# Second mixer of a two-layer encoder: key norms spread as fp32r pairs, the last value block bank by bank, six unread products at the first statistics

## The reference

```
x = x + 0.5 * swiglu(rms_norm(x, ffn1_norm[layer]), ...)
x = x + mixer(rms_norm(x, mix_norm[layer]), ...)      # layer 0: Hyena and windowed attention; layer 1: RWKV-7
x = x + 0.5 * swiglu(rms_norm(x, ffn2_norm[layer]), ...)
```

```
r, k, v = xr @ w_r, xk @ w_k, xv @ w_v
decay, a = f(xw @ w1 @ w2), sigmoid(a0 + xa @ a1 @ a2)          # per direction, low rank
kk = k * k_k                                                    # 16 heads of 64 channels
kk = kk / max(norm(kk over the 64 channels of a head), 1e-12)
k_dir, b_dir = k * (1 + (a - 1) * k_a), kk * a                  # per direction
S = S * w + (S @ -kk) outer b_dir + v outer k_dir               # scan over positions, both directions
```

## Time and profile before

| | us |
|---|---|
| median of 3 runs | 1233.02 |
| lowest and highest | 1231.18, 1236.94 |
| the profiled execution | 1231.86 |
| its span in the trace | 1230.1 |

### The profile page before, as it was taken

One profiled execution on the slowest core, in us unless ns is written; L12 is line 12 of the kernel. 1 busy time (PEld: TensorE's weight loads), 2 busy tenths in 40 slices (PEclk: granted clock), 3 DMA queues, 4 the chain that ended last, 5 costly groups with the idle time before them and its releaser, 6 DMA issues.

```text
span 1230.1 us, 27474 instructions
## 1 busy us (share of the span) xinstructions
PE 1198.3 (97%) x11198; PEld 1085.7 (88%) x11198; DVE 793.2 (64%) x1259; ACT 654.7 (53%) x1116; POOL 403.3 (33%) x218
## 2 busy tenths in 40 slices
PE   8999999998999999999999989998999999999998
PEld 6899999877889999998999979987999889999998
DVE  7655554787585555575555569969777758755554
ACT  5545454655274454475445446684666654554452
POOL 0343433212113434423443410006344412344433
PEclk9999999999999999999999989999999999999999
DMA  9345455422254554555455444421000025554452
GB/s 364 123 187 191 168 204 201 155 106 99 108 198 173 193 191 169 203 206 205 168 190 190 171 151 155 167 92 54 3 4 3 3 75 190 205 201 176 182 202 89
DMA packets 18657, 188.04 MB, mean 153 GB/s; under 512 B 2064, under 2 KB 2576, under 8 KB 3600
## 3 DMA queue, kind: packets, MB, share of 16 engines
q1 hardware_dynamic: 18576, 186.87, 41.3%
HBM read 185.82 MB, written 1.05 MB: 152 GB/s over the span
## 4 chain that ended last, share of the span: by engine, by line
PE 83%; DVE 10%; ACT 5%; issue 1%; DMA 0%; SPq 0%; DVEq 0%; ACTq 0%
PE gu_bank L267 24%; PE gu_bank L269 12%; PE bank L246 7%; PE bank L248 7%; PE bank L247 7%; PE bank L1493 7%; PE gu_bank L246 3%; PE gu_bank L1493 3%; PE gu_bank L247 3%; PE gu_bank L248 3%; DVE WL L201 2%; PE gu_bank L1524 2%; ACT WH L189 2%; DVE HX L407 1%; PE bank L949 1%
## 5 line engine op out<-in xcount | busy, mean ns | idle before, releaser
L210 POOL TENSOR_TENSOR WL<-raw,WH 128x1024 fp32r<-128x1024 f32 x96 | 325.8, 3393 | 587.9 <-ACT WH L195 566.4
L267 PE MATMUL gu_bank<-HX,WH 128*128 128x512 f32 x1280 | 455.7, 399 | 1.1 <-DVE PL L548 1.1
L269 PE MATMUL gu_bank<-HX,WL 128*128 128x256 f32 x1280 | 359.5, 281 | 0.0
L201 DVE TENSOR_TENSOR WL<-raw,WH 128x2048 fp32r<-128x2048 f32 (+1 forms) x113 | 242.8, 2148 | 123.3 <-ACT WH L189 123.3
L267 PEld LDWEIGHTS gu_bank<-HX,WH 128*128 128x128 f32 x1280 | 240.7, 188 | 57.4 <-DVE PL L548 1.7
L269 PEld LDWEIGHTS gu_bank<-HX,WL 128*128 128x128 f32 x1280 | 242.0, 189 | 0.0
L189 ACT ACTIVATE WH<-raw 128x2048 fp32r<-128x2048 f32 (+1 forms) x113 | 203.0, 1797 | 23.8 <-PE gu_bank L248 14.4
L246 PE MATMUL bank<-PH,WH 128*128 128x256 f32 (+1 forms) x720 | 202.3, 285 | 0.0
L247 PE MATMUL bank<-PL,WH 128*128 128x256 f32 (+1 forms) x720 | 201.7, 283 | 0.0
L248 PE MATMUL bank<-PH,WL 128*128 128x256 f32 (+1 forms) x720 | 201.6, 283 | 0.0
L246 PE MATMUL gu_bank<-HX,WH 128*128 128x256 f32 x464 | 137.2, 296 | 3.9 <-DVE HX L407 3.0
(11 more groups left out here) (319 smaller groups left out, 1810.8 us busy)
## 6 DMA issues: line engine op xcount, KB each, us to landing
raw<-stream_in SPq DMA_DIRECT2D x114, 1536.0 KB, 6.3
cst<-const_in SPq DMA_DIRECT2D x1, 1600.0 KB, 17.2
X<-xT_in SPq DMA_DIRECT2D x1, 1024.0 KB, 5.4
raw<-stream_in SPq DMA_DIRECT2D x1, 1024.0 KB, 7.4
arena<-hconst_in SPq DMA_DIRECT2D x2, 512.0 KB, 10.8
out<-X SPq DMA_DIRECT2D x4, 256.0 KB, 2.1
arena<-hconst_in SPq DMA_DIRECT2D x1, 768.0 KB, 13.9
arena<-fw_in SPq DMA_DIRECT2D x1, 512.0 KB, 8.2
```

Of the source, the lines that this page charges most:

```text
L201: nc.vector.tensor_tensor(WL[:, slot, :cut], raw[:, slot, :cut], WH[:, slot, :cut].bitcast(fp32), ALU.subtract).then_inc(lo_ready, 1)
L210: (eng or nc.gpsimd).tensor_tensor(WL[:, slot, cut:end], raw[:, slot, cut:end], WH[:, slot, cut:end].bitcast(fp32), ALU.subtract).then_inc ...
L267: nc.tensor.matmul(out[:, :], WH[:, slot, w:w + P], HX[:, x, :, :].rearrange("p i t -> p (i t)"), start=k == 0, stop=False)
L269: return nc.tensor.matmul(out[:, L:2 * L], WL[:, slot, w:w + P], HH[:, x, :], start=False, stop=k == CT - 1)
```

## The change

Three edits. (1) Ahead of the first statistics PE issues six products of `ones` with itself, 128 columns each, into columns 0 to 127 of `bank[3]`, which the statistics' product then overwrites; no one reads them, and they come ahead of the wait for the sums. (2) The reciprocal norms are split into a high and a low fp32r part (`RNH` by ACT, `RNL` by DVE) and `selt` is copied to an fp32r tile (`SELR`, by ACT), all in the upper half of `HX`. Each of the eight spreads is then two fp32r products, and the eight are issued in four groups: tiles 0 and 1 in v5 where all eight stood, tiles 2 and 3, 4 and 5, 6 and 7 ahead of the first three output pairs of v6. DVE waits for all eight before its first write of scan operands. (3) In v7 the output tiles come in the order 6, 7, 2, 3, 4, 5, 0, 1, each pair raises `v_done`, and ACT copies each bank after its own pair.

```diff
+        def pe_keep(pe, out, moving, n):
+            for _ in range(n):
+                nc.tensor.matmul(out, ones, moving, start=True, stop=True)
         def pe_stats(pe, n):
+            if n == 0:
+                pe_keep(pe, stats_bank(n)[:, 0:P], ones, 6)
             pe.wait_ge(sum_ready, n + 1 if n < 4 else n)
...
+        V_COPIES = (3, 1, 2, 0)
+        spent = HX[0:16, 4:8, :, :].rearrange("p k i t -> p (k i) t")
+        RNH, RNL, SELR = spent[:, 2, :], spent[:, 3, :], spent[:, 4:8, :].rearrange("p j (i c) -> p (j i) c", c=P)
...
-            for m in range(CT):
+            final = outs is VB and k == CT - 1
+            for n in range(CT):
+                m = 2 * V_COPIES[n // 2] + n % 2 if final else n
...
-                if m == CT - 1:
+                if n == CT - 1:
                     last.then_inc(blocks_done, 1)
+                elif final and n % 2:
+                    last.then_inc(v_done, 1)
...
-        def pe_spread_norms(pe):
-            pe.wait_ge(kk_rec, 1)
-            pe.wait_ge(lr_ready, 32)
-            for j in range(CT):
-                nc.tensor.matmul(pair_half(XB, j), selt[:, j, :], RN[:, 1, :], start=True, stop=True).then_inc(kk_bc, 1)
+        def pe_spread_norms(pe, js):
+            if js[0] == 0:
+                pe.wait_ge(kk_parts, 3)
+                pe.wait_ge(lr_ready, 32)
+            for j in js:
+                nc.tensor.matmul(pair_half(XB, j), SELR[:, j, :], RNH, start=True, stop=False, skip_group_check=True)
+                nc.tensor.matmul(pair_half(XB, j), SELR[:, j, :], RNL, start=False, stop=True, skip_group_check=True).then_inc(kk_bc, 1)
...
                     if k == 5:
-                        wait = lambda n: pe_spread_norms(pe) if n == 3 else None
+                        wait = lambda n: pe_spread_norms(pe, (0, 1)) if n == 3 else None
+                    if k == 6:
+                        wait = lambda n: pe_spread_norms(pe, (2 * n + 2, 2 * n + 3)) if n < 3 else None
...
# act_mix1
                 if n == 8:
+                    act.wait_ge(kk_rec, 1)
+                    A(RNH, RN[:, 1, :], cp).then_inc(kk_parts, 1)
+                    A(SELR, selt, cp).then_inc(kk_parts, 1)
                     hidden()
...
-            act.wait_ge(blocks_done, 3 * S_O)
-            for j in (3, 1, 2, 0):
+            for n, j in enumerate(V_COPIES):
+                act.wait_ge(v_done, n + 1) if n < 3 else act.wait_ge(blocks_done, 3 * S_O)
                 A(V[:, 2 * j * L:2 * (j + 1) * L], VB[j][:, :], cp).then_inc(va_read, 1)
...
# dve_mix1
+                if n == 9:
+                    dve.wait_ge(kk_parts, 2)
+                    tt(RNL, RN[:, 1, :], RNH.bitcast(fp32), ALU.subtract).then_inc(kk_parts, 1)
...
             dve_kb_wait(dve, 0)
+            dve.wait_ge(kk_bc, CT)
             own(dve_b(0, 0, 0))
```

More of the change, by code:

```diff
@@ L1317, in build @@
         omk_ready = sem("omk_ready")
+        kk_parts = sem("kk_parts")
         hid_ready = sem("hid_ready")
@@ L1345, in build @@
         LEAD = 4
+        V_COPIES = (3, 1, 2, 0)
+        v_done = sem("v_done")
         WINDOW = {2: (6, 7, 8), 3: (9, 10), 4: (11, 12), 5: (13, 14), 6: (15, 16), 7: (17, 18), 8: (19, 20), 9: (21, 22, 23)}
+        spent = HX[0:16, 4:8, :, :].rearrange("p k i t -> p (k i) t")
+        RNH, RNL, SELR = spent[:, 2, :], spent[:, 3, :], spent[:, 4:8, :].rearrange("p j (i c) -> p (j i) c", c=P)
         KB, RB4, VB = bank[4:8], bank[0:4], [bank[6], bank[7], bank[0], bank[1]]
```

## The result

The changed kernel takes 1237.25 us (median of 7 runs, 1235.01 to 1238.59), the kernel before 1234.64 (7 runs, 1231.18 to 1236.94): 1.0029 of before, interval 1.0015 to 1.0043. By the ratio it is slower by some 3.6 us, by the medians by 2.6; 1230.2 was forecast, and the range ended at 1233.7. The forecast was built on the first three runs of the kernel before, whose median was 1233.02; from 1234.64 the same gain of 2.8 us would lead to 1231.8, so that the baseline explains 1.6 us of the miss and no more.

What follows compares the result with a forecast made beforehand. PE was taken to bound the kernel (83% of the chain), with DVE deciding at scan tile 0. Gains of 1.7 us at the opening and 1.1 at tile 0 sum to 2.8, giving 1230.2 us; range 1227.2 to 1233.7.

Steps and rivals of the forecast that it cites:

- The new wait: At DVE's first L1850, before tile 0: waiting for all eight spreads holds DVE 0.2 us, paid in full.
- rival (c): DVE's wait for the eighth spread: at 0.47 us per spread product, a net loss of 2.8 us, 1235.8; chance 0.05.
- Where that gain goes: At scan tile 0: PE comes early, DVE's masks decide, running back to back; 1.3 us gained, not 3.3.
- The 1.1 us of gain forecast at tile 0: At scan tile 0: 1.3 us gained at the masks less 0.2 us of DVE's wait.
- the half clock at v6: PE's products of v5 to v7 behind the spreads: 1.59 us lost to half clock, expected to go.
- Opening: Before the first statistics: six products of 0.25 us fill PE's wait at no cost; the clock holds, gaining 1.69 us.
- rival (a): At the opening the clock falls anyway or had not always fallen; 1.1 us of gain left, 1231.9; chance 0.25.
- the stages behind wait for PE or move with it: Behind the opening: later stages follow PE, so its 1.69 us gain there was counted in full.
- The copies and the preparation: ACT's two copies and DVE's subtraction before the spreads hidden, 0 us; last value block's early copies 0 beside the pairs.
- The 0.9 us given to it alone: Last value block's new order and early copies, if standing alone: 0.9 us, DVE's idle time before its first mask.

Runs made afterwards that it cites:

- pairs_only: The kernel before with the second edit alone (spreads as pairs in four groups, their preparation, DVE's wait for all eight): 1.0019 of before.
- changed_no_keep: The changed kernel without the six unread products: 1.0028 of before.
- late_wait: The changed kernel with spread weights of tiles 0 to 3 and 4 to 7 swapped, so DVE needs all eight only behind `dve_b` and `dve_k`: 0.9998 of before.
- together: The changed kernel with all eight spread pairs in one group inside v5: 0.9986 of before.
- copies_only: The kernel before with the third edit alone (last value block by banks, early copies): 0.9996 of before.
- keep_only: The kernel before with the six unread products alone: 1.0007 of before.
- late_wait_no_keep: Four spread groups with DVE's wait 1.5 us later and copies by banks, without the six unread products: 0.9985 of before.

## Why the prediction was wrong

**"The new wait", the step that failed.** DVE's wait for the eighth spread was forecast at 0.2 us and paid back one for one; the price that rival (c) gave it, dearer products, did not come (0.12 us each). Its size was missed twice. First, a change of operand height costs 0.10 us on both sides of it: the product behind the first one of a new height is late too (827.18 to 827.40 and 827.84 to 828.06 are 0.22 where 0.12 is usual). A group with six products takes 1.57 us, not 1.39; all 16 cost (832.56 - 827.09) - 18 x 0.12 = 3.3 us, not 2.64. DVE was 0.89 us late at L1850, not 0.2. A product of that kind was in my hands (828.73, 0.39 long, in the earlier trace rows). Second, and larger, I took DVE's chain as rigid: 0.2 us in, 0.2 us out. At the masks it came out 0.89 + 1.54 = 2.4 us later. At the query product, for which PE waits, it came out 0.89 + 3.24 = 4.1 us later (7.64 - 4.40 is 3.24). The three traces with the early wait (changed, pairs_only, changed_no_keep) all have 3.98 us for the query product, 1.84 for `dve_k` (L1873 after) and 1.29 for `dve_alpha`; the eleven traces without it have 2.3, 0.75 and 0.75. POOL's operations fall otherwise beside them in the two groups of traces. That the delay is what changes the order is shown by late_wait; what makes POOL and DVE take turns otherwise once DVE is late was not isolated.

**"Where that gain goes" was right** as long as the chain is on time: PE comes first, DVE decides, and the masks run without idle time (late_wait, together). What I did not price is what a late query product does to a PE that is early. Ready at 837 and idle to 840.66, it lost the clock for 6.8 us, and its first two halves took 6.5 us in place of 3.9. The clock fell at 838 to 840 us in all three traces with the early wait and in none of the other eleven. Of the 17.72 - 13.6 = 4.1 us by which this mixer is longer than one with the chain on time and full clock, 2.4 are DVE's delay at the masks, and the other 1.7, by subtraction, the clock's. The 1.1 us of gain forecast at tile 0 became a loss of 17.72 - 15.43 = 2.3 us against the trace before.

**The baseline of that step.** I priced the half clock at v6 as part of the kernel. It is there in some executions only, and costs 0, 1.8 or 3.4 us (13.6, 15.4, 17.0): in four of the seven traces that have the eight float32 spreads. In the five traces with four groups of pairs the clock never falls at the spreads, which is what the prediction expected of them; with the 16 in one block it fell in one of two.

**Opening: rival (a), and a cost that I did not have.** The six take 0.26 us each (0.25 forecast), the clock holds, and the stretch is 1.5 us shorter in the trace. That this is their doing isn't shown. Of nine profiled executions without them (or their like) the clock fell at 26 to 28 us in four only. In three it had fallen at 15 to 16 us already, and in pairs_only and copies_only it did not fall in the opening at all; pairs_only needs 11.46 us there without the six, as the changed kernel does with them (11.47). In all five with them it fell at 288 to 300, where it never did in the nine. This took back 1.7 us in the changed kernel's trace (at 299.9) and some 0.5 in keep_only's (at 288.4). Whether the second is caused by the first isn't settled. And the longer code cost 2 us in waits, though I had "the stages behind wait for PE or move with it". In the three pairs with and without the six (changed, together, late_wait) they cost 0.1, 0.5 and 1.6 us by the ratios, and -0.6, 1.0 and 0.4 by the distances from before, each with an interval of over 2 us to either side. So the gain of 1.7 is not there, and a cost of about 0.5 is likely but not shown.

**The copies and the preparation were right:** ACT's two copies ended 0.53 us ahead of need with DVE's subtraction in its gap, and the order of the copies alone moved nothing that can be measured (0.9996). The 0.9 us given to it alone was not seen, within an interval 3.7 us wide, and the mixers of 13.63 and 13.64 us with and without it say that there is none at full clock. In the changed kernel the copies (L2163) began at 836.06, not at 832.3, because ACT had to wait for DVE's late L1873; they still ended before DVE came to the masks.

**The sum:** forecast -2.8 us, measured +3.6 by the ratio. The early wait is worth some 4 to 5 us of the difference of 6.4 (3.7 to 5.3, changed against together and late_wait, with and without the six), and the six products some 2 (a gain of 1.7 that did not come, and a small cost). What is left over, with the wait moved and without the six, is 1.3 to 1.9 us faster than before (late_wait_no_keep): close to the 1.1 forecast for the other edits, and in part by luck, since the half clock at v6 that stood in that sum is not in every execution of the kernel before.

## What to carry to other kernels

When an engine that shares its work with another gets a new wait, price not the wait but the order in which the two engines' operations then fall: here 0.9 us of waiting became 4.1 at the product for which PE waits and 2.4 at the masks, and some 4 us of time with the clock. Put a reuse wait ahead of the first write that needs it, not of the first write in the region: moving it by two operations, by laying the early-freed data under the early writer, won some 4 us. Judge a fall of the clock by several executions before paying for its cure.

## What had not been expected

- Instructions that do no work changed the time of stages 340 us and more behind them: 0.5 to 1.0 us at a third step, at places that change with what was added (24 waits, 72 waits, or products). The path goes through transfers that land later; why they do is open.
- The clock's falls wander from execution to execution: at 829 us, 0, 3.4 or 6.8 us of half clock in the same code of the second mixer, in kernels that differ elsewhere.
- 16 rows in fp32r cost what 128 do, 0.12 us a product; a block of 16 of them is cheap, four blocks of four are not, by 0.2 us a change of height.
